# Level products of a chunked recurrence as two 64-row tiles per head pair, pool weights as 64x64 tiles

## The chip, the cores and the metric

One core of one Trainium2 chip. The metric is the time of one execution in microseconds (us) on the device. Engines are named as in the profile: PE (TensorE, with PEld for its weight loads), DVE (VectorE), ACT (ScalarE), POOL (GpSimd), SP (SyncE, which issues the DMAs).

## What is computed

One layer of a hybrid decoder on 2048 tokens of width 1024. The part that the change touches is the gated recurrence (four heads of 64) and the pooling mixer. The recurrence works in chunks of 64 tokens with a decay between each pair of tokens of a chunk:

```python
def step(state, inp):                       # one chunk, all heads
    q_, k_, v_, g_ = inp
    b = jnp.cumsum(g_, axis=2)
    o_inter = jnp.einsum('bhck,bhkv->bhcv', q_ * jnp.exp(b), state)
    diff = b[:, :, :, None, :] - b[:, :, None, :, :]
    decay = jnp.where(causal, jnp.exp(jnp.where(causal, diff, 0.0)), 0.0)
    scores = jnp.einsum('bhik,bhjk,bhijk->bhij', q_, k_, decay)
    o = o_inter + jnp.einsum('bhij,bhjv->bhiv', scores, v_)
    ...
# pooling mixer: y = einsum('bsgc,gcd->bsgd', pooled, w_grp), four groups of 64 channels
```

Around it stand the input projection (16 column tiles of 128), sliding-window attention (8 heads of 64), an output projection, and a gated feed-forward layer of width 2816 with a short convolution.

## The kernel before, in words

Tokens are worked in four blocks of 512. `one_block(0, True)` is written out and also loads and splits the weights; blocks 1 to 3 run as one loop body. Each block goes through input projection with the recurrence's and the attention's small products between its units, output projection, and feed-forward layer. Each engine runs its own program in the order in which the code is written; nothing schedules them, and they meet at semaphores.

Large products are three matmuls of 512 columns (high*high, high*low, low*high) at L606 to L608 (weights stationary) and L631 to L633 (activations stationary). They are of type f32r. The small products are plain float32, and each such matmul stands as two instructions in the trace, with a weight load (LDWEIGHTS) of its own.

**The level products.** The scores inside a chunk come from six levels, of halves of 32, 16, 8, 4, 2 and 1 tokens: within each group of 2w tokens the keys of the first half meet the queries of the second. On DVE `level_sub` (L1491) writes the differences of the cumulative decay to `ZB`, ACT takes exponentials (L1119, L1120), `level_mul` multiplies the second halves by the queries into `ZR` (L1500) and the first halves by the keys into `ZB` (L1503), `level(o)` on PE makes the product (L704), and `level_take` copies it under a mask into `A` (L1520). The 128 partitions hold two heads of 64. To get two heads' products from one matmul over 128 rows, `ZR` is block-diagonal: for each group of 128 tokens it has 128 columns, 64 for each head, and zeros in the other head's half. L1500 thus runs twice a level, on 64 partitions each, and the zeros are written once a block (L1570). A level has 8 matmuls (4 token tiles by 2 head pairs), 16 instructions. `level(0)` (L709, 2 columns) makes the diagonal.

In PE's order the levels stand between the units of the input projection: levels 0 and 1 ahead of unit 7, level 2 ahead of unit 8, level 3 ahead of unit 9, level 4 ahead of unit 10, level 5 behind it and followed by `chunk_states` (L739, 64x64 tiles), level 6 between `scores(0)` and `scores(1)` (L724, whole array, then L728, tiles of 64 rows by 128 columns). `recurrence` follows (L804, whole array; L813, 64x64 tiles). In block 0 `ada_rows` (L548, tiles of 32 columns) runs after units 7, 8, 9 and 10, hence just ahead of levels 2, 3, 4 and 5.

**Pooling.** `pooling` runs two matmuls of 512 columns with a block-diagonal `PW` (L793), into banks 6 and 7 of `ps`, between output units 1 and 2; ACT (L1080) and DVE (L1469, L1470) turn the result into operands of output unit 3.

Of the kernel before, what the change touches and what calls it, by code (L numbers as in the profile page):

```python
# [14 lines left out]
P = 128  # L15
D = 1024
S = 2048
BT = 512
# [53 lines left out]

ACT_STEPS, DVE_STEPS, UP_STEPS = 28, 105, 16

# [23 lines left out]
def hymba_block(nc, x, c, w_ada, b_ada, g_pre_mix, g_post_mix, w_in, hg_norm, pool_w, pool_scale,  # L98
# [19 lines left out]
    with ctx:  # L118
# [83 lines left out]
        ZB = sb("ZB", [P, 2, 2 * BT], fp32, early)  # L202
        ZR = sb("ZR", [P, 2, 2 * TT, P], fp32, early)
        early.close()
# [9 lines left out]
        def fb(name, shape, dt=fp32):  # L214
# [25 lines left out]
              quarter(A[:].rearrange("p t h n -> p (t h n)")), AQ[:], quarter(ZB[:].rearrange("p a n -> p (a n)")),  # L240
              quarter(ZR[:].rearrange("p a b n -> p (a b n)")), AWQK[:], AWT[:], AWG[:])
        DG = AWT[:].rearrange("p k (a n) -> p (k a) n", n=P)
# [285 lines left out]
        def _(pe):  # L528
# [63 lines left out]
            def one_block(b, first):  # L592
# [95 lines left out]
                def level(o, tok):  # L688
# [11 lines left out]
                    for t in range(TT):  # L700
                        for j in range(2):
                            if o:
                                col = (2 * (t % 2) + j) * P
                                ins = mm(ps[:, 4 + 2 * (o % 2) + t // 2, col:col + P],  # L704
                                         ZB[:, (o - 1) % 2, j * BT + t * P:j * BT + t * P + P],
                                         ZR[:, (o - 1) % 2, j * TT + t, :], start=True, stop=True)
                            else:
                                col = 4 * t + 2 * j
                                ins = mm(ps[:, 4, col:col + 2], R[:, j, t * P:t * P + P], hsel[:], start=True, stop=True)  # L709
# [79 lines left out]
                def pooling():  # L789

                    fenced(s["pool_ready"], b + 1)
                    for a in range(2):
                        ins = mm(ps[:, 6 + a, :], PW[:, a, :], R[:, a, :], start=True, stop=True)  # L793
                    ins.then_inc(s["pool_mm"], 1)
# [582 lines left out]
        def _(dve):  # L1377
# [80 lines left out]
            def one_block(b, first):  # L1458
# [35 lines left out]
                def level_mul(l):  # L1494
                    w = LEVELS[l]
                    dve.wait_ge(s["lev_exp"], b * 12 + 2 * l + 2)
                    z, q, k = (y.rearrange("p (n w) -> p n w", w=2 * w) for y in (ZB[:, l % 2, :], flat(Q), flat(K)))
                    for par in range(2):
                        r = slice(64 * par, 64 * par + 64)
                        step(tt(ZR[r, l % 2, :, r].rearrange("p a (n w) -> p a n w", w=w),  # L1500
                                z[r, :, w:2 * w].rearrange("p (a n) w -> p a n w", a=2 * TT),
                                q[r, :, w:2 * w].rearrange("p (a n) w -> p a n w", a=2 * TT), ALU.mult))
                    tt(z[:, :, 0:w], z[:, :, 0:w], k[:, :, 0:w], ALU.mult).then_inc(s["z_ready"], 1)  # L1503

                def level_take(o):
# [9 lines left out]
                    for g in range(2):  # L1515
                        src = ps[:, 4 + 2 * (o % 2) + g, :].rearrange("p (a n w) -> p a n w", a=8, w=w)
                        dst = A[:, 2 * g:2 * g + 2, :, :].rearrange("p t h (n w) -> p (t h) n w", w=2 * w)[:, :, :, w:2 * w]
                        m = hgmask[:, o - 1, :].rearrange("p (n w) -> p n w", w=w)\
# [26 lines left out]
                def window_sums(a):  # L1545
# [21 lines left out]
                    .then_inc(s["kdd"], 1)  # L1567
                for par in range(2):

                    step(ts(ZR[64 * par:64 * par + 64, :, :, 64 * (1 - par):64 * (1 - par) + 64]  # L1570
                            .rearrange("p a b n -> p (a b) n"),
                            ident[64 * par:64 * par + 64, 64 * (1 - par):64 * (1 - par) + 64].unsqueeze(1)
                            .to_broadcast([64, 4 * TT, 64]), 0.0, None, ALU.mult))
                dve.wait_ge(s["q_softplus"], b + 1)
# [206 lines left out]
```

## Time and profile before

| | |
|---|---|
| time of the kernel before | 2347.45 us, median of 3 (2346.28 to 2348.02) |
| the profiled execution | 2343.45 us, its span 2341.7 us |
| PE busy | 2275.6 us (97%), weight loads 1837.2 us |
| DVE busy | 1256.7 us (54%) |
| ACT, POOL busy | 772.3 us (33%), 229.4 us (10%) |
| mean granted TensorE clock | 0.992 |

A row of the chain of work gives start, length and line of each piece of the chain that ended last. For PE a piece runs from the end of the instruction before to its own end, so it is what that instruction added. The single durations of matmuls and weight loads are longer, since they overlap.

### The profile page before, as it was taken

The numbers are of one execution on the slowest core, as the hardware profiler recorded it, in microseconds if no ns is written. First come the engines' busy times: TensorE is split into PE (matmuls) and PEld (weight loads), VectorE is DVE, ScalarE is ACT, GpSimd is POOL, SyncE is SP. The second block draws the span as 40 slices with busy tenths as digits, with TensorE's granted clock in tenths as the row PEclk, the third lists the DMA queues.
The fourth block names the chain that finished last, engine by engine and source line by source line (L and its number), as shares of the span: only waits on it lengthen the run. The fifth ranks groups of instructions, "written<-read, shape, count | busy, mean of one in ns | idle before, by whom it ended". The sixth has DMA issues, their size and how long they took to land.

```text
span 2341.7 us, 33056 instructions
## 1 busy us (share of the span) xinstructions
PE 2275.6 (97%) x11291; PEld 1837.2 (78%) x11307; DVE 1256.7 (54%) x2145; ACT 772.3 (33%) x1500; POOL 229.4 (10%) x151
## 2 busy tenths in 40 slices
PE   6999899999999999999999999999999999999997
PEld 4776688788788778888888778888888877888886
DVE  3648484675766555152556745334355665515345
ACT  3535433343344432121134532113024344212212
POOL 2322244444300000000000000000000000000000
PEclk9999999999999999999999999999999999999999
DMA  9963688878563446555564254655546334655555
GB/s 362 353 223 137 223 293 301 283 272 300 212 256 112 144 145 249 187 191 197 188 221 150 73 198 167 233 194 196 196 163 235 109 144 156 226 193 197 194 187 193
DMA packets 115396, 483.14 MB, mean 206 GB/s; under 512 B 7999, under 2 KB 38985, under 8 KB 69705
## 3 DMA queue, kind: packets, MB, share of 16 engines
q1 hardware_dynamic: 115273, 481.53, 56.8%
q8 instruction: 73, 1.20, 0.2%
q14 instruction: 50, 0.41, 0.1%
HBM read 378.74 MB, written 102.76 MB: 206 GB/s over the span
## 4 chain that ended last, share of the span: by engine, by line
PE 90%; DVE 5%; issue 1%; DMA 1%; SPq 1%; ACT 1%; DVEq 0%; ACTq 0%
PE ps L606 18%; PE ps L608 18%; PE ps L607 18%; PE ps L631 8%; PE ps L633 8%; PE ps L632 8%; PE ps L704 2%; PE ps L728 1%; PE ps L839 1%; PE ps L827 1%; PE ps L670 1%; PE ps L548 1%; PE ps L804 1%; SPq L291 1%; DMA AWT<-in_w_ada_dram 1%
## 5 line engine op out<-in xcount | busy, mean ns | idle before, releaser
L606 PE MATMUL ps<-hTh,wt 128*128 128x512 f32 x1920 | 758.4, 395 | 12.9 <-DVE hTl L1470 8.7
L608 PE MATMUL ps<-hTh,wt 128*128 128x512 f32 x1920 | 748.4, 390 | 0.0
L607 PE MATMUL ps<-hTl,wt 128*128 128x512 f32 x1920 | 748.1, 390 | 0.0
L606 PEld LDWEIGHTS ps<-hTh,wt 128*128 128x128 f32 x1920 | 360.9, 188 | 105.5 <-issue 26.8
L608 PEld LDWEIGHTS ps<-hTh,wt 128*128 128x128 f32 x1920 | 360.7, 188 | 76.3
L607 PEld LDWEIGHTS ps<-hTl,wt 128*128 128x128 f32 x1920 | 361.2, 188 | 71.5
L1704 DVE TENSOR_SCALAR cv<-ub,CW 128x512 f32<-128x512 f32 x176 | 98.2, 558 | 472.5 <-ACT ub L1315 458.0
L1315 ACT ACTIVATE ub<-ps 128x512 f32<-128x512 f32 x176 | 105.3, 598 | 689.7 <-PE ps L608 689.7
L631 PE MATMUL ps<-wt,pTh 128*128 128x512 f32 x704 | 275.1, 391 | 1.9 <-ACT T L1082 1.9
L633 PE MATMUL ps<-wt,pTh 128*128 128x512 f32 x704 | 274.0, 389 | 0.0
L632 PE MATMUL ps<-wt,pTl 128*128 128x512 f32 x704 | 273.9, 389 | 0.0
L511 POOL TENSOR_TENSOR wt<-raw,wt 128x1024 fp32r<-128x1024 f32 x88 | 214.6, 2446 | 402.7 <-ACT wt L989 363.1
L1706 DVE SCALAR_TENSOR_TENSOR cv<-ub,CW,cv 128x512 f32<-128x512 f32 x176 | 162.0, 920 | 26.8 <-DVE halo L1705 26.8
L1707 DVE SCALAR_TENSOR_TENSOR cv<-ub,CW,cv 128x512 f32<-128x512 f32 x176 | 143.1, 813 | 24.8
L631 PEld LDWEIGHTS ps<-wt,pTh 128*128 128x128 f32 x704 | 132.2, 188 | 29.3 <-issue 2.3
L633 PEld LDWEIGHTS ps<-wt,pTh 128*128 128x128 f32 x704 | 132.2, 188 | 27.6
L632 PEld LDWEIGHTS ps<-wt,pTl 128*128 128x128 f32 x704 | 132.2, 188 | 27.0
L1743 DVE TENSOR_TENSOR Y<-Y,ps 128x512 f32<-128x512 f32 x64 | 43.3, 687 | 170.8 <-PE ps L633 170.8
L989 ACT ACTIVATE wt<-raw 128x1024 fp32r<-128x1024 f32 x92 | 95.1, 1036 | 58.7 <-PE ps L633 41.1
L1325 ACT ACTIVATE pTh<-P 128x512 f32 (+1 forms) x88 | 55.3, 628 | 155.7 <-DVE P L1713 155.7
L1500 DVE TENSOR_TENSOR ZR<-ZB,Q 64x512 f32<-64x512 f32 x48 | 35.1, 730 | 73.5 <-ACT ZB L1120 72.3
L1718 DVE TENSOR_TENSOR pTl<-P,pTh 128x512 f32 x88 | 60.6, 688 | 13.6 <-ACT pTh L1325 13.6
(243 smaller groups left out, 2350.3 us busy)
## 6 DMA issues: line engine op xcount, KB each, us to landing
wt<-split_w SPq DMA_DIRECT2D x268, 1024.0 KB, 4.8
split_w<-wt SPq DMA_DIRECT2D x88, 1024.0 KB, 7.0
raw<-in_w_up_dram SPq DMA_DIRECT2D x22, 1024.0 KB, 9.6
XT<-in_w_ada_dram SPq DMA_DIRECT2D x10, 1024.0 KB, 11.5
XN<-in_x_dram SPq DMA_DIRECT2D x5, 2048.0 KB, 9.2
raw<-in_w_in_dram SPq DMA_DIRECT2D x8, 1024.0 KB, 13.7
XR<-in_x_dram SPq DMA_DIRECT2D x4, 2048.0 KB, 10.3
raw<-in_w_down_dram SPq DMA_DIRECT2D x8, 1024.0 KB, 9.2
```

The source lines that it names most:

```text
L511: pool.tensor_tensor(lo, src, hi.bitcast(fp32), ALU.subtract).then_inc(s["w_lo"], 1)
L606: mm(ps[:, bank, :], w, hTh[:, k, :], start=(k == 0), stop=False)
L607: mm(ps[:, bank, :], w, hTl[:, k, :], start=False, stop=False)
L608: ins = mm(ps[:, bank, :], wl[:, slot, k, :], hTh[:, k, :], start=False, stop=(k == KD - 1))
L631: mm(ps[:, 4 * n + t, :], h, flat(wh, j), start=f, stop=False)
L632: mm(ps[:, 4 * n + t, :], l, flat(wh, j), start=False, stop=False)
L633: ins = mm(ps[:, 4 * n + t, :], h, flat(wl, j), start=False, stop=e)
L989: act.activation(hi, src, ACT.Copy).then_inc(s["w_hi"], 1)
L1315: act.activation(ub[:, u, 2:], ps[:, u, :], ACT.Copy).then_inc(s["acc_taken"], 1)
L1704: up(ts(cv[:, u, :], ub[:, u, 2:], tap(2), tap(3), ALU.mult, ALU.add))
L1706: up(stt(cv[:, u, :], ub[:, u, 1:BT + 1], tap(1), cv[:, u, :], ALU.mult, ALU.add))
L1707: stt(cv[:, u, :], ub[:, u, 0:BT], tap(0), cv[:, u, :], ALU.mult, ALU.add)\
```

## The change

`ZR` loses its zero half: it is 64 columns for each token tile and head pair, with head 0 on partitions 0 to 63 and head 1 on 64 to 127. `level_mul` writes it with one instruction on 128 partitions. The L1570 zeroing is gone. On PE each matmul over 128 rows with 128 moving columns becomes two over 64 rows with 64 moving columns, one in each half of the rows, with weights of 64x128; the two heads of a pair write two different banks, where before the banks went by token tiles. `level_take` reads and writes the same number of elements in the new order. `pooling` runs four matmuls on diagonal 64x64 tiles instead of two; both tiles of a pair write the same bank, on different partitions. A buffer of the first block's loads (`AWZ`) takes the place that it had in `ZR`.

```diff
@@ level(), PE
-    col = (2 * (t % 2) + j) * P
-    ins = mm(ps[:, 4 + 2 * (o % 2) + t // 2, col:col + P],
-             ZB[:, (o - 1) % 2, j * BT + t * P:j * BT + t * P + P],
-             ZR[:, (o - 1) % 2, j * TT + t, :], start=True, stop=True)
+    col = (2 * t + j) * 64
+    for par in range(2):
+        r = slice(64 * par, 64 * par + 64)
+        ins = mm(ps[:, 4 + 2 * (o % 2) + par, col:col + 64],
+                 ZB[r, (o - 1) % 2, j * BT + t * P:j * BT + t * P + P],
+                 ZR[r, (o - 1) % 2, j * TT + t, :], start=True, stop=True)
@@ pooling(), PE
-    ins = mm(ps[:, 6 + a, :], PW[:, a, :], R[:, a, :], start=True, stop=True)
+    for q in range(2):
+        r = slice(64 * q, 64 * q + 64)
+        ins = mm(ps[r, 6 + a, :], PW[r, a, r], R[r, a, :], start=True, stop=True)
@@ level_mul(), DVE
-    for par in range(2):
-        r = slice(64 * par, 64 * par + 64)
-        step(tt(ZR[r, l % 2, :, r]..., z[r, :, w:2 * w]..., q[r, :, w:2 * w]..., ALU.mult))
+    step(tt(ZR[:, l % 2, :, :].rearrange("p a (n w) -> p (a n) w", w=w),
+            z[:, :, w:2 * w], q[:, :, w:2 * w], ALU.mult))
@@ level_take(), DVE
-    dst = A[:, 2 * g:2 * g + 2, :, :].rearrange("p t h (n w) -> p (t h) n w", w=2 * w)[:, :, :, w:2 * w]
+    dst = A[:].rearrange("p t h n -> p (t h) n").rearrange("p (a par) (n w) -> p par a n w", par=2, w=2 * w)\
+        [:, g, :, :, w:2 * w]
@@ one_block(), DVE
-    for par in range(2):
-        step(ts(ZR[64 * par:64 * par + 64, :, :, 64 * (1 - par):64 * (1 - par) + 64]..., 0.0, None, ALU.mult))
```

Nothing changes its place in any engine's order. On PE, in the loop body of blocks 1 to 3, before unit 9's first products, level 3 of before (`REGISTER_ALU` rows are waits on a register's value):

```order
1797 L697 REGISTER_ALU
1798 L704 MATMUL ps<-ZR,ZB 128x128 x8
1799 L649 REGISTER_ALU
1800 L606 MATMUL ps<-hTh,wt 128x512
1801 L607 MATMUL ps<-hTl,wt 128x512
```

and of the change:

```order
1797 L700 REGISTER_ALU
1798 L709 MATMUL ps<-ZR,ZB 128x64 x16
1799 L652 REGISTER_ALU
1800 L609 MATMUL ps<-hTh,wt 128x512
1801 L610 MATMUL ps<-hTl,wt 128x512
```

The neighbours stay; eight products of 128 columns are sixteen of 64. On PE at level 6, between the attention's scores (identity and mask L724, keys L728), before:

```order
1870 L724 MATMUL ps<-bmask,identb 128x512 x2
1871 L728 MATMUL ps<-KT,AQ 128x256 x4
1872 L782 ISA
1873 L693 REGISTER_ALU
1874 L704 MATMUL ps<-ZR,ZB 128x128 x8
1875 L724 MATMUL ps<-bmask,identb 128x512 x2
1876 L728 MATMUL ps<-KT,AQ 128x256 x4
```

and with the change:

```order
1870 L729 MATMUL ps<-bmask,identb 128x512 x2
1871 L733 MATMUL ps<-KT,AQ 128x256 x4
1872 L787 ISA
1873 L696 REGISTER_ALU
1874 L709 MATMUL ps<-ZR,ZB 128x64 x16
1875 L729 MATMUL ps<-bmask,identb 128x512 x2
1876 L733 MATMUL ps<-KT,AQ 128x256 x4
```

Here the level stands behind products of 64 rows, whose shape it now shares, and ahead of a product on the whole array. On PE at the pooling, between output units 1 and 2, before and then with the change:

```order
2078 L633 MATMUL ps<-wt,ATT 128x512
2079 L896 REGISTER_ALU
2080 L793 MATMUL ps<-R,PW 128x512 x2
2081 L864 REGISTER_ALU
2082 L631 MATMUL ps<-wt,hTh 128x512
```

```order
2078 L636 MATMUL ps<-wt,ATT 128x512
2079 L903 REGISTER_ALU
2080 L800 MATMUL ps<-R,PW 64x512 x4
2081 L871 REGISTER_ALU
2082 L634 MATMUL ps<-wt,hTh 128x512
```

Two products on the whole array are four on quarters of it, between products on the whole array.

## Rows read from the trace of the kernel before

**Rows 1.** The page: busy times, and the chain's shares by engine.
```profile
PE 2275.6 (97%) x11291; PEld 1837.2 (78%) x11307; DVE 1256.7 (54%) x2145; ACT 772.3 (33%) x1500; POOL 229.4 (10%) x151
...
PE 90%; DVE 5%; issue 1%; DMA 1%; SPq 1%; ACT 1%; DVEq 0%; ACTq 0%
```

**Rows 2.** The chain in block 1, levels 0, 1, 3, 5 (start, us, what).
```profile
690.04 1.68 PE ps L709 x16
691.73 1.89 PE ps L704 x16
693.62 0.23 PE ps L606
...
706.83 1.79 PE ps L704 x16
708.62 0.23 PE ps L606
...
723.16 1.79 PE ps L704 x16
724.95 1.14 PE ps L739 x62
```

**Rows 3.** The chain in block 1 from the chunk states to the recurrence.
```profile
726.08 0.43 PE ps L606
...
733.58 1.06 PE ps L728 x8
734.64 0.03 issue
734.67 2.02 PE ps L704 x16
736.70 0.43 PE ps L724 x2
...
746.04 1.09 PE ps L813 x64
747.14 0.43 PE ps L606
```

**Rows 4.** Groups of PEld by form (rows by columns of the load; busy us, mean ns).
```profile
L704 PEld LDWEIGHTS ps<-ZR,ZB 128*128 128x128 f32 x384 | 47.0, 196 | 6.7 <-issue 5.7
...
L728 PEld LDWEIGHTS ps<-KT,AQ 64*128 64x128 f32 x256 | 22.0, 186 | 15.0 <-issue 13.5
L839 PEld LDWEIGHTS ps<-PT,VA 128*64 128x64 f32 x256 | 15.6, 136 | 10.7 <-issue 5.8 <-DVE ATT L1542 0.4
...
L739 PEld LDWEIGHTS ps<-VH,KDT 64*64 64x64 f32 x256 | 4.3, 134 | 0.5
```

**Rows 5.** Timeline of PEld, 733.505 to 733.6 us.
```profile
733.51 0.19 PEld L728 LDWEIGHTS ps<-KT,AQ 64*128 64x128 f32 x2 [0.42 <-issue]
```

**Rows 6.** Groups of DVE by form (count, busy us, mean ns, idle before).
```profile
L1500 DVE TENSOR_TENSOR ZR<-ZB,Q 64x512 f32<-64x512 f32 x48 | 35.1, 730 | 73.5 <-ACT ZB L1120 72.3
...
L1503 DVE TENSOR_TENSOR ZB<-ZB,K 128x512 f32<-128x512 f32 x24 | 16.6, 693 | 0.8
...
L1570 DVE TENSOR_SCALAR ZR<-ident 64x1024 f32<-64x1024 f32 x8 | 7.7, 961 | 0.1
```

**Rows 7.** Timeline of DVE in block 1: level 3's operands, and the states.
```profile
700.92 1.41 DVE L1500 TENSOR_TENSOR ZR<-ZB,Q 64x512 f32<-64x512 f32 x2 [1.68 <-ACT ZB L1120]
702.36 0.69 DVE L1503 TENSOR_TENSOR ZB<-ZB,K 128x512 f32<-128x512 f32 x1
...
730.99 3.45 DVE L1599 SCALAR_TENSOR_TENSOR SS<-SS,EB,ps 128x64 f32<-128x64 f32 x11 [0.18 <-DVE SS L1599]
```

**Rows 8.** The chain in block 1 at the pooling.
```profile
802.36 1.72 PE ps L793 x4
804.08 0.23 PE ps L631
```

**Rows 9.** Timeline of DVE behind the pooling in block 1.
```profile
806.44 0.69 DVE L1470 TENSOR_TENSOR hTl<-T,hTh 128x512 fp32r<-128x512 f32 x1
```

**Rows 10.** The chain in block 0, levels 2 to 5.
```profile
106.92 1.98 PE ps L704 x16
110.28 0.79 PE ps L557 x8
...
117.66 0.60 SPq L291
...
118.30 12.66 DMA AWG<-in_w_ada_dram
...
132.94 3.30 PE ps L704 x16
...
146.30 1.98 PE ps L704 x16
```

**Rows 11.** Timeline in block 0, from level 2 to that load: ACT, POOL, SP.
```profile
111.10 0.17 ACT L1058 ACTIVATE MOD<-ps 128x4 f32<-128x4 f32 x1 [3.52 <-PE ps L557]
...
112.39 2.39 POOL L511 TENSOR_TENSOR wt<-raw,wt 128x1024 fp32r<-128x1024 f32 x1 [8.42 <-ACT wt L989]
...
114.81 0.83 SPq L325 DMA_DIRECT2D split_w<-wt  x2
```

**Rows 12.** Stretches: busy of PE, PEld, DVE, ACT, POOL, then PEclk, the granted clock.
```profile
265.00:271.30 6.30, 3.56 (x19) 2.61 (x19) 6.03 (x7) 6.04 (x17) 0.00 (x0) 1.00 0.78 257
834.20:840.50 6.30, 3.63 (x20) 2.67 (x18) 5.85 (x8) 5.85 (x17) 0.00 (x0) 1.00 0.57 199
...
272.20:275.60 3.40, 3.40 (x18) 3.26 (x16) 1.13 (x2) 1.19 (x2) 0.00 (x0) 0.50 0.00 0
840.00:843.40 3.40, 2.87 (x24) 2.59 (x24) 1.23 (x2) 2.05 (x5) 0.00 (x0) 1.00 0.74 287
1398.60:1402.00 3.40, 3.03 (x14) 3.03 (x15) 1.07 (x2) 1.33 (x4) 0.00 (x0) 0.50 0.65 270
1958.40:1961.80 3.40, 3.15 (x15) 3.15 (x16) 0.95 (x2) 1.21 (x4) 0.00 (x0) 0.50 0.62 236
```

More of the change, by code:

```diff
@@ L71, in ada_use @@
     return slot, sum(s == slot for p in ADA_SLOT[:e] for s in p) + 1
-ACT_STEPS, DVE_STEPS, UP_STEPS = 28, 105, 16
+ACT_STEPS, DVE_STEPS, UP_STEPS = 28, 97, 16
 def place(u):
@@ L202, in hymba_block @@
         ZB = sb("ZB", [P, 2, 2 * BT], fp32, early)
-        ZR = sb("ZR", [P, 2, 2 * TT, P], fp32, early)
+        wide = ExitStack()
+        AWZ = sb("AWZ", [P, 4, 512], fp32, wide)
+        wide.close()
+        ZR = sb("ZR", [P, 2, 2 * TT, P // 2], fp32, early)
         early.close()
@@ L240, in hymba_block @@
               quarter(A[:].rearrange("p t h n -> p (t h n)")), AQ[:], quarter(ZB[:].rearrange("p a n -> p (a n)")),
-              quarter(ZR[:].rearrange("p a b n -> p (a b n)")), AWQK[:], AWT[:], AWG[:])
+              AWZ[:], AWQK[:], AWT[:], AWG[:])
         DG = AWT[:].rearrange("p k (a n) -> p (k a) n", n=P)
@@ L1497, in level_mul @@
                     z, q, k = (y.rearrange("p (n w) -> p n w", w=2 * w) for y in (ZB[:, l % 2, :], flat(Q), flat(K)))
-                    for par in range(2):
-                        r = slice(64 * par, 64 * par + 64)
-                        step(tt(ZR[r, l % 2, :, r].rearrange("p a (n w) -> p a n w", w=w),
-                                z[r, :, w:2 * w].rearrange("p (a n) w -> p a n w", a=2 * TT),
-                                q[r, :, w:2 * w].rearrange("p (a n) w -> p a n w", a=2 * TT), ALU.mult))
+                    step(tt(ZR[:, l % 2, :, :].rearrange("p a (n w) -> p (a n) w", w=w),
+                            z[:, :, w:2 * w], q[:, :, w:2 * w], ALU.mult))
                     tt(z[:, :, 0:w], z[:, :, 0:w], k[:, :, 0:w], ALU.mult).then_inc(s["z_ready"], 1)
@@ L1567, in one_block @@
                     .then_inc(s["kdd"], 1)
-                for par in range(2):
[L1570 to L1573, printed above, removed]
                 dve.wait_ge(s["q_softplus"], b + 1)
```

## The prediction, made before the change was run

> **What bounds the kernel now.** I read the page first. PE is busy 97% of the span, and 90% of the chain of work that ended last is PE [rows 1]. So PE's own order is the path, and the question is what each product adds to it. I then read the chain in block 1, where nothing but PE stands in it from the levels to the recurrence. There a level adds 1.79 us for 16 instructions, 0.112 us each, and the projection's next product, L606, adds its ordinary 0.23 us [rows 2]. Level 0 adds 1.68 us for 16, or 0.105 us each, although only 2 columns move through the array where the other levels move 128 [rows 2]. So the moving columns do not set the pace of a small product: what both have in common is a weight load of 128 columns. The loads' durations say by what they go: 186 ns for 64 rows by 128 columns and 196 for 128 by 128, but 136 for 128 by 64 and 134 for 64 by 64 [rows 4]. Columns count, rows do not.
>
> DVE is busy 54% [rows 1]. In the levels it stands idle ahead of L1500, 72.3 us in all, until ACT's exponentials come [rows 6], and none of it is in the chain there. Its result is early: level 3's operands are done at 703.05 (702.36 + 0.69) [rows 7], and PE comes to that level at 706.83 [rows 2].
>
> **Part 1, DVE.** 48 instructions of 730 ns (35.1 us) become 24 on 128 partitions. The same form exists in L1503, 693 ns [rows 6]: 16.6 us. The zeroing, 7.7 us, goes. DVE loses 26.2 us of 1256.7, some 6.5 a block. Worth on the path: nothing at levels 2 to 5, where the operands are already 3.8 us early in the example above. The one place where DVE comes close is the chunk states, which end at 734.44 (730.99 + 3.45) [rows 7], when PE waits for them ahead of level 6 at 734.67 [rows 3]. The last L1500 stands ahead of them on DVE, so they come 0.7 us earlier. I count that under level 6. `level_take` moves as many elements as before: nothing.
>
> **Part 2, the steady rate of a level.** A level becomes 32 instructions, 16 pairs. The two of a pair use different rows. Do they overlap? L728 is the nearest row: 64 rows by 128 columns of weights, two row halves, 256 columns moving. Two such loads stand within 0.19 us, the length of one [rows 5], and eight products take 1.06 us, 0.13 each [rows 3]. At twice L704's columns they could not take less than 0.22 each if they ran one behind another. So pairs overlap. Each pair still needs a load of 128 columns, the same as one instruction of before. I take 0.112 us a pair, hence 1.79 us a level: **no gain and no loss** at the steady rate. The ends: half of it (0.9 us) if rows counted in a load, twice (3.58 us) if the two ran in turn; both are rivals below.
>
> **Part 3, changing the shape of the tiles.** Here the change costs. Wherever PE goes from tiles to the whole array, the next product adds 0.43 us, not 0.23: behind L739 and behind L813 [rows 3]. Behind an untiled level it adds 0.23 [rows 2]. Leaving tiles costs **0.20 us**. Entering a new shape: a level behind L728 takes 2.02 us [rows 3] where one behind L608 takes 1.79 [rows 2], so 0.23 us, in which the first load and the first moving columns are laid bare. With 64 columns moving for 128 about 0.05 of it goes, and 0.03 may be waiting (the issue row ahead of it [rows 3]). I take **0.14 us** for entering tiles of 64 rows, with 0 and 0.23 as ends. The Trainium skill has this as a rule, in "TensorEngine Tiling (Array Packing)", section Key Properties: changing the tiling mode drains the engine, while going from tile to tile does not. The trace agrees, with the 0.20 and 0.23 us just read. By the same rule level 6 saves its entry behind L728, as the next list has it from the rows; were tiles of any shape free to change, level 5 and L739 would share one drain and the sum would be 0.6 us less.
>
> In blocks 1 to 3:
> - Level 1 stands behind level 0, and its 1.89 us already show 0.10 us of a bare load [rows 2]. Entering adds 0.04, leaving 0.20: 0.24.
> - Levels 2, 3 and 4 stand between products on the whole array: 3 x 0.34 = 1.02.
> - Level 5 enters (0.14); it was followed by a change of shape before (L739) and still is: 0.14.
> - Level 6 follows L728, whose shape it now has: its 2.02 us fall to 1.79, -0.23, and the states that PE waited for are earlier. But L724 on the whole array follows; leaving costs 0.17 there, a little under 0.20 since its own load is of bf16 (a guess between 0.14 and 0.20). Together -0.06.
> - Pooling: four instructions of 512 columns take 1.72 us, 0.43 each [rows 8]. Eight on diagonal quarters, in pairs that overlap, take the same; entering and leaving add 0.34. The split of its result ends at 807.13 (806.44 + 0.69) [rows 9]; output unit 3 begins 24 products of 0.227 us behind 804.08 [rows 8], at 809.5. 2.4 us of cover hold the added time, the more so as both shift together.
>
> That is 1.68 us a block, 5.04 for three.
>
> Block 0 differs, as L548's tiles of 32 columns stand ahead of levels 2 to 5: those levels pay for a change of shape already (1.98 us at 106.92 and 146.30 [rows 10], 0.19 over 1.79) and save the 0.05 of the shorter columns. Level 1: 0.24. Level 2: -0.05 + 0.20 = 0.15; it is not hidden, since L557 behind it, at 110.28, leads through ACT, POOL and SP [rows 11] to the load at 118.30. Level 3 lies under that load of 12.66 us [rows 10]: 0. Level 4 runs at half clock, 3.30 us [rows 10]: 0.2, within 0.15 and 0.3. Level 5: -0.05. Level 6: -0.06. Pooling 0.34. Together 0.82.
>
> **The sum:** 5.04 + 0.82 = 5.9 us. Against the profiled execution's 2343.45 us that is 2349.3. The median of the runs is 4.0 us above that execution, a difference that the change leaves alone: 2347.45 + 5.9 = **2353.3 us**, 0.25% slower. Bounds: with every entry at nothing (16 places at 0.14 and four at 0.04 less) the sum is 3.5 us; with 0.23 at the 16 places it is 7.3.
>
> **Rivals.**
>
> *The pool's pairs run in turn* (slower still). The two quarters of a pair write one bank. No row shows that: L728, L739 and L813 send different row halves to different banks. If they must take turns, 8 x 0.43 = 3.44 us for 1.72, so 1.72 x 4 = 6.9 us more: 2360.2. For it: nothing in the trace, either way. Against: the two write different partitions, and L739 with two column halves in one bank overlaps (62 in 1.14 us [rows 2]). The Trainium skill, in "TensorEngine Tiling (Array Packing)", section Gotcha 1: PSUM Pressure, says that different row tiles cannot use one PSUM bank at the same time. No run here shows whether the hardware then waits.
>
> *Rows count in a load* (the other side: faster). Then a pair takes 0.056 us, a level 0.9, and 23 levels on the path save 0.89 each, 20.5 us: 2347.45 + 5.9 - 20.5 = 2332.9. It decides from the point where a pair takes less than 0.10 us. Against it stands 186 ns for a load of 64 rows beside 134 with half the columns [rows 4], and level 0's 0.105 us at 2 columns. The Trainium skill, in "TensorEngine Tiling (Array Packing)", section Theoretical Speedup, gives up to 2x for a small dimension of 64 or less, which is this case; by the same rows the trace speaks against it here.
>
> *The pairs of a level run in turn.* 23 levels x 1.79 = 41 us: 2394. Against: the overlap of L728 [rows 3, 5].
>
> *The clock hides it* (no measurable change). Ahead of the feed-forward layer PE is busy only 3.56 of 6.3 us in block 0, and 3.63 of 6.3 in block 1 [rows 12]. In block 0 the granted clock is then 0.50 (1.2 GHz) for a stretch of 3.4 us, and so in blocks 2 and 3; in block 1 it stays 1.00 (2.4 GHz) [rows 12]. Whether it falls after much the same idle is thus a matter of when that comes, and the change moves when. A stretch at half clock costs up to 1.7 us of PE. Two or three of them gone give back 3 to 5 us: 2349 or so. One more gives 2355.
>
> **How the numbers follow.** My forecast has 0.69, with a range of its own of 2350.5 to 2356.5. The pool in turn has 0.13, the clock 0.11, rows in a load 0.04, level pairs in turn 0.03. The range of 8 in 10 reaches from 2349.5, the clock's case, to 2360.5, the pool's. A measurement of this kernel tells 0.2% (4.7 us) from no change, so the border to slower is 2352.1, only 1.2 us under my forecast. Of the forecast's 0.69 I put 0.48 above it and 0.20 below, of the clock's case all between, with 0.01 of luck left to faster. Slower 0.48 + 0.13 + 0.03 = 0.64, faster 0.04 + 0.01 = 0.05, within 0.2% 0.31.
>
> **What would show it.** In the chain of the profile after: levels 2 to 4 at 1.93 us each with the next L606 line at 0.43; level 6 near 1.79 and the L724 behind it about 0.6 for the two; pooling near 1.86 us and the next product 0.43; DVE some 26 us less busy, with more idle ahead of `ZR`. Pooling at 3.5 us shows the bank. A level under 1.5 or over 2.3 us shows my steady rate wrong. If the rows are as I say and the time is still 2349 or less, I look for the stretches at half clock, and then for a wait that DVE's relief took away which I read as covered.

## The result, and the profile after

| | before | after |
|---|---|---|
| median of five executions | 2347.45 us (2345.70 to 2348.02) | 2357.54 us (2355.51 to 2362.76) |
| ratio, interval of 95% | | 1.0049 [1.0036, 1.0062] |
| the profiled execution, its span | 2343.45, 2341.7 us | 2355.51, 2353.8 us |
| its granted clock, mean | 0.992 | 0.989 |
| granted clock, mean of the five executions | | 0.988 |

The change makes the kernel 0.49% slower: 10.1 us between the medians, 12.1 between the profiled executions. It lies in the predicted range (2349.5 to 2360.5), but above the predicted time of 2353.3 and outside the forecast's own range (2350.5 to 2356.5): 5.9 us were forecast and some 10 came.

The page after, beside [rows 1] and [rows 6] (a group's row: engine, operation, tiles and count | busy us, mean ns | idle time ahead of it and what ended it):

```profile
PE 2288.7 (97%) x11691; PEld 1843.3 (78%) x11707; DVE 1231.8 (52%) x2113; ACT 771.9 (33%) x1500; POOL 228.9 (10%) x151
...
L1505 DVE TENSOR_TENSOR ZR<-ZB,Q 128x512 f32<-128x512 f32 x24 | 16.6, 692 | 98.1 <-ACT ZB L1127 97.7
```

DVE is 24.9 us less busy, and its idle time ahead of this line, now L1505, has grown from 72.3 to 97.7 us: what DVE saves it waits for ACT, one for one. The prediction had 26.2 us less; `level_mul`'s multiplication into `ZB`, an instruction whose form did not change, takes 18.7 us in all where it took 16.6.

The level products are now L709, level 0 is L714, the projection's products L609 to L611, the masks L729, the pooling L800. The chain of work in block 1 (start, length, line), beside [rows 2, 3, 8]:

```profile
693.51 1.68 PE ps L714 x16
695.19 1.93 PE ps L709 x32
697.12 0.43 PE ps L609
...
702.79 1.93 PE ps L709 x32
704.72 0.43 PE ps L609
...
727.87 1.93 PE ps L709 x32
729.81 1.14 PE ps L744 x62
...
738.42 1.06 PE ps L733 x8
739.49 1.73 PE ps L709 x32
741.22 0.54 PE ps L729 x2
...
806.95 1.86 PE ps L800 x8
808.82 0.43 PE ps L634
```

Level by level this is close to what was forecast. The difference of these rows against those of before is 0.24 for level 1, 3 x 0.34 for levels 2 to 4, 0.14 for level 5, 1.73 - 2.02 + 0.54 - 0.43 = -0.18 for level 6 and 0.34 for the pooling: 1.56 us a block, where the prediction had 1.68. And the weight loads show why a level became no faster: 64 rows of 128 columns take 197 ns, where 128 rows of 128 took 196 [rows 4].

```profile
L709 PEld LDWEIGHTS ps<-ZR,ZB 64*128 64x128 f32 x768 | 47.7, 197 | 8.6 <-issue 8.4
```

Three blocks at 1.56 us and block 0 at some 0.8 make 5.5 us of shape changes. More than half of the 12.1 us between the profiled executions is still to be found. Most of it is in the same lines, at other places. Block 3 and block 0 after (the same view):

```profile
1815.92 1.68 PE ps L714 x16
1817.60 2.99 PE ps L709 x32
1820.59 0.72 PE ps L609
1821.31 0.43 PE ps L610
```

```profile
117.93 1.41 SPq L294
...
119.39 12.73 DMA AWG<-in_w_ada_dram
...
132.16 1.93 PE ps L551 x8
134.10 3.61 PE ps L709 x32
137.71 0.72 PE ps L609
...
139.28 1.71 PE ps L684 x8
...
142.27 0.86 PE ps L560 x8
```

The same place of before, behind [rows 10]:

```profile
138.52 0.78 PE ps L557 x8
```

Stretches of both kernels (busy of PE, PEld, DVE, ACT, POOL, then the granted clock). After, levels 0 and 1 of block 3, which begin at 1815.9:

```profile
1814.00:1818.20 4.20, 4.20 (x37) 3.87 (x37) 0.35 (x1) 2.13 (x4) 0.00 (x0) 1.00 0.28 62
1818.20:1825.00 6.80, 6.80 (x35) 5.72 (x34) 5.78 (x6) 2.02 (x4) 0.00 (x0) 0.50 0.27 116
```

Block 0 behind the wait for `AWG`, first after, then before:

```profile
128.70:135.50 6.80, 5.27 (x30) 1.90 (x32) 0.81 (x2) 0.60 (x1) 0.00 (x0) 0.50 1.05 392
135.50:142.40 6.90, 6.90 (x39) 6.10 (x37) 2.56 (x3) 0.00 (x0) 0.00 (x0) 0.51 0.04 17
```

```profile
128.80:135.60 6.80, 5.73 (x29) 2.93 (x22) 1.05 (x2) 0.60 (x1) 0.00 (x0) 0.50 1.03 384
135.60:142.50 6.90, 6.90 (x46) 6.11 (x46) 2.54 (x3) 2.66 (x6) 1.87 (x1) 1.00 0.01 5
```

The granted clock falls to 0.50 (1.2 GHz) in the midst of busy PE work in block 3, 0.6 us into level 1, and in block 2 too (3.4 us from 1258.5, 0.5 us behind the end of level 1). In block 0 both kernels fall to 0.50 while PE waits for `AWG` and runs `ada_rows`; before comes back to 1.00 behind level 4, and after stays at 0.50 for twice as long. Outside the last 13 us of the span, before has 23.9 us at 1.2 GHz and after 41.0.

I priced each such stretch by its own rows: every PE product in it against its length at 2.4 GHz. That makes 8.5 us before and 14.2 after, 5.7 more. This is an estimate; in experiments with more such stretches the terms come to 0.5 to 2 us more than the span.

The rows put the 5.7 us at places. Behind the landing of `AWG` it is 2.7 us, of which about 0.3 is the change of shape. At levels 0 and 1 it is about 1.6 us in block 2 and 3.0 in block 3. The other stretches, which lie partly elsewhere than before, give back some 1.3.

With the shapes' 5.5 that makes 11.2. The remaining 0.9 us is the wait for `AWG`: from the end of `ada_rows` to the landing it is 13.30 us before (130.96 - 117.66) and 14.19 after (132.12 - 117.93). In the ten experiments it is 14.2 to 14.8 us, also where nothing in block 0's levels 2 to 5 is tiled (14.77 in `e_level0_twice`). So the tiles are not needed for it, and the profiled execution of before was quick there.

**A price for the mean clock.** The mean clock of an execution is recorded with its time. I took the 93 of the experiments' kernels and of the runs of before beside them. One line through all, with an offset for each kernel and, for before, for each of its three sets, has a slope of 1.34 us for 0.001 of the mean clock and leaves 1.3 us. With it the kernels can be put at one clock, 0.992. This is an estimate, and good to about 1 us. Before stands at 2345.1, 2345.2 and 2344.2 then, and after, by its five times, at 2352.3: some 7.1 us. The rest, some 3 to 4 us, is clock.

### The profile page after: what moved, and what is told of

It reads as the page before. It is cut to its first block, busy times and chain, and to the rows that moved or that the text cites. A ratio compares the mean times of both kernels' runs of the same rounds, so it can differ in the third digit from the quotient of the medians.

```text
span 2353.8 us, 33796 instructions
## 1 busy us (share of the span) xinstructions
PE 2288.7 (97%) x11691; PEld 1843.3 (78%) x11707; DVE 1231.8 (52%) x2113; ACT 771.9 (33%) x1500; POOL 228.9 (10%) x151
## 4 chain that ended last, share of the span: by engine, by line
PE 90%; DVE 5%; issue 1%; DMA 1%; SPq 1%; ACT 1%; DVEq 0%; ACTq 0%
PE ps L609 18%; PE ps L611 18%; PE ps L610 18%; PE ps L634 8%; PE ps L635 8%; PE ps L636 8%; PE ps L709 2%; PE ps L733 1%; PE ps L846 1%; PE ps L834 1%; PE ps L673 1%; PE ps L551 1%; PE ps L811 1%; SPq L294 1%; PE ps L684 1%
## 5 line engine op out<-in xcount | busy, mean ns | idle before, releaser
L609 PE MATMUL ps<-hTh,wt 128*128 128x512 f32 x1920 | 760.2, 396 | 11.5 <-DVE hTl L1477 8.3
L611 PE MATMUL ps<-hTh,wt 128*128 128x512 f32 x1920 | 749.7, 390 | 0.0
L609 PEld LDWEIGHTS ps<-hTh,wt 128*128 128x128 f32 x1920 | 361.5, 188 | 104.8 <-issue 24.7
L611 PEld LDWEIGHTS ps<-hTh,wt 128*128 128x128 f32 x1920 | 361.5, 188 | 76.7
L1505 DVE TENSOR_TENSOR ZR<-ZB,Q 128x512 f32<-128x512 f32 x24 | 16.6, 692 | 98.1 <-ACT ZB L1127 97.7
```

The costliest lines, as they stand in the source:

```text
L609: mm(ps[:, bank, :], w, hTh[:, k, :], start=(k == 0), stop=False)
L611: ins = mm(ps[:, bank, :], wl[:, slot, k, :], hTh[:, k, :], start=False, stop=(k == KD - 1))
```

## The experiments

Each kernel ran four to ten times beside the kernel before, in three groups, each on a chip of its own. The text quoted under a heading is what was expected before that run. The column "1.2 GHz" is the sum of the stretches at 0.50 in the profiled execution, without the end of the span; "cost" what they took from PE, priced as above. The first group is the four rows from `e_split01` to `e_levels_only`, the second `e_after_again` and the three from `e_pe_only` to `e_quarters`, the third the last two rows. The figures of before stand in the order of the groups.

| kernel | median (range), us | ratio to before | at clock 0.992 | 1.2 GHz, cost |
|---|---|---|---|---|
| before, beside the three groups | 2345.55, 2347.04, 2345.70 | | 2345.1, 2345.2, 2344.2 | 23.9, 8.5 |
| after | 2357.54 | 1.0049 [1.0036, 1.0062] | 2352.3 | 41.0, 14.2 |
| e_after_again | 2355.70 (2355.11 to 2356.73) | 1.0038 [1.0024, 1.0051] | 2351.5 | 44.4, 14.4 |
| e_split01 | 2352.78 (2350.4 to 2355.9) | 1.0034 [1.0021, 1.0047] | 2350.6 | 27.3, 8.5 |
| e_level1_only | 2359.02 (2358.59 to 2364.73) | 1.0061 [1.0048, 1.0074] | 2354.0 | 47.8, 16.6 |
| e_not_level1 | 2353.52 (2349.68 to 2357.2) | 1.0033 [1.0023, 1.0042] | 2348.9 | 41.0, 11.2 |
| e_levels_only | 2354.01 (2349.54 to 2357.86) | 1.0032 [1.0019, 1.0045] | 2349.2 | 47.8, 15.6 |
| e_pe_only | 2357.53 (2351.03 to 2362.1) | 1.0048 [1.0034, 1.0062] | 2350.7 | 34.1, 11.5 |
| e_block0_level4 | 2353.24 (2349.41 to 2358.22) | 1.0024 [1.0013, 1.0036] | 2349.4 | 51.2, 16.6 |
| e_quarters | 2330.87 (2328.51 to 2335.32) | 0.9933 [0.992, 0.9947] | 2329.2 | 30.7, 9.4 |
| e_quarters_split | 2330.17 (2327.81 to 2330.98) | 0.9929 [0.9915, 0.9942] | 2329.2 | 34.1, 9.7 |
| e_level0_twice | 2373.00 (2366.63 to 2375.0) | 1.0117 [1.0101, 1.0132] | 2362.9 | 44.4, 17.5 |

The theory: PE pays for each change of the tiles' shape, and the rest of the loss is the clock, which falls or stays down where tiled level products run. Its rivals: the fallen stretches are chance, DVE's or the pooling's part of the change is behind the rest, or a term of the shapes is larger than its row.

### Level 1 away from level 0

On the kernel after:

```diff
     level(0, 2)
-    level(1, 2)
-    unit(7)
+    unit(7, {4: lambda: level(1, 2)})
```

> The changed kernel with one edit: level 1's products leave their place right behind level 0 and stand in the middle of projection unit 7 (behind 4 of its 8 k-tiles). Theory 1 (the quiet stretch): half of the loss of 10 us comes from the granted clock, which falls to 1.2 GHz because level 0 (1.68 us with 2 columns moving) and the tiled level 1 (1.93 us) stand in a row. Then no stretch at half clock is left at level 0 or 1 in blocks 1 to 3, and the time is 2353 to 2355 us. Theory 2 (phase): stretches at half clock fall where they do by the time at which idle comes, not by this pair; then this edit changes nothing systematic and the time stays 2356 to 2359 us with stretches at half clock at either level in some blocks. Both expect the level's own products to take 1.93 us plus 0.20 us for leaving the tiles.

The chain in block 1:

```profile
693.97 1.34 PE ps L714 x12
695.31 0.35 PE ps L609
...
698.20 1.93 PE ps L709 x32
700.13 0.43 PE ps L609
```

Level 1 costs the same wherever it stands (1.93 and 0.43), and leaving level 0's two columns for the large product adds 0.12. No stretch at 0.50 lies in or behind levels 0 and 1 in any block, and the cost of the clock is that of before, 8.5 us. The profiled execution is 5.1 us shorter than that of after. The medians say less: 2352.78, just under the first theory's 2353 to 2355, against 2357.54 and 2355.70, with intervals of the ratio that overlap.

### One level alone, and all but that one

Both start from the kernel before; the levels named read 64-row halves of its block-diagonal operand, the others are whole. DVE's multiplication and the pooling stay as before.

```diff
@@ level()
-    if o:
+    if o in (1,):            # e_not_level1: (2, 3, 4, 5, 6)
+        col = (2 * t + j) * 64
+        for par in range(2):
+            r = slice(64 * par, 64 * par + 64)
+            ins = mm(ps[:, 4 + 2 * (o % 2) + par, col:col + 64],
+                     ZB[r, (o - 1) % 2, j * BT + t * P:j * BT + t * P + P],
+                     ZR[r, (o - 1) % 2, j * TT + t, r], start=True, stop=True)
+    elif o:
```

> The kernel before with one part of the change: level 1 alone runs as two products of 64 rows per head pair, read out of the block-diagonal operand, which stays with all its work on DVE; its result is copied in the new bank order. The chain of the change prices this at 0.04 + 0.20 us a block, 1.0 us in all. Theory 1 (quiet stretch of level 0 and tiled level 1): in some of blocks 1 to 3 the clock falls to 1.2 GHz there, and the time is 2351 to 2353.5 us. Theory 2 (phase, or any tiled product alike): 2348 to 2349.5 us.

> The counterpart: the kernel before with levels 2 to 6 tiled and level 1 and the pooling as they were, the block-diagonal operand and its DVE work kept. By the price of changing shape: 5.9 - 1.0 (level 1) - 1.4 (pooling) = 3.5 us over before, 2351. Theory 1: that is all, since level 1 is whole behind level 0: 2350.5 to 2352, no stretch at half clock at level 0 and 1 in blocks 1 to 3. Theory 2 (any tiled level adds its share of the clock's loss, 4 us over 6 levels): 2353.5 to 2355.

By the sum's terms, level 1 alone should cost 1.0 us and the others 3.5. At equal clock the others do: 2348.9 against 2345.1, 3.8. Their profiled execution has no fall at levels 0 and 1 either. But the median, 2353.52, is 8.0 us over before, above the first theory's range and at the edge of the second's, and equal clock takes out just what the two differ in. Of the ten executions five took 2349.7 to 2351.8 us at a clock of 0.989 to 0.991 and five 2355.2 to 2357.2 at 0.987; the profiled one is of the first five. The mean clock, 0.9887, is as low as that of the whole change (0.9878 and 0.9888). So a clock loss of some 3.7 us is there with level 1 whole, and more of it than block 0's stretch. Where it lies in the longer executions no profile shows.

Level 1 alone missed both ranges. It costs 8.9 us at equal clock and 13.5 in the medians, more than the whole change. Its rows say where. The first 60 us have a stretch of 17.1 us at 1.2 GHz (from 34.4), and PE has fallen 4.4 us behind before at 51 us, ahead of any level. One fall (3.4 us from 1826.4) begins as level 1 of block 3 ends. The largest part is a wait that no theory had: 3.6 us of "issue" or more at each of the two jumps back to the head of the loop (up to 1217.7 and 1782.1), where before has 0.5 at most. Each has a stretch at 1.2 GHz beside it, of which this is the first:

```profile
1218.80:1222.20 3.40, 3.40 (x10) 2.62 (x9) 3.37 (x4) 0.50 (x3) 0.00 (x0) 0.51 0.64 251
```

The kernel can't be read as the price of level 1.

### Levels without the pooling

The kernel after, with the pool's products of before:

```diff
-    for q in range(2):
-        r = slice(64 * q, 64 * q + 64)
-        ins = mm(ps[r, 6 + a, :], PW[r, a, r], R[r, a, :], start=True, stop=True)
+    ins = mm(ps[:, 6 + a, :], PW[:, a, :], R[:, a, :], start=True, stop=True)
```

> The changed kernel with the pooling back as two products on the whole array. Both theories: 4 x 0.34 us less than the change, 2355.5 to 2357, and the pooling's four instructions at 1.72 us again with 0.23 us for the next product.

2354.01 us, under the 2355.5 to 2357 that was expected. At equal clock it stands 4.1 us over before, where the terms without the pooling's 1.4 give 4.5. The pooling in block 0 (now L798) is back at its old rows:

```profile
236.05 1.72 PE ps L798 x4
237.77 0.23 PE ps L634
```

Its profiled execution is as long as that of after (spans of 2353.7 and 2353.8 us), with 15.6 us of clock for 14.2. The pooling itself is settled by the rows, 1.86 and 0.43 us with the change. Its pairs, on one bank, overlap.

### The change again

> The changed kernel unchanged, once more, beside the next ones on one chip. Shapes cost 5.9 us, which a run pays at any clock; the rest is clock. 2354 to 2359 us, median 2356. Theory 1a: the tiled level 4 in block 0 again leaves the clock at 1.2 GHz for about 13.7 us from 129 us on, where before it was 6.8. Theory 1b: in some of blocks 1 to 3 the clock falls at level 0 and 1.

2355.70 us, 1.8 under the first set. The stretches at 1.2 GHz are nearly the same in sum (44.4 and 41.0 us), but not in place. Block 2's levels stay at 1.00 this time, and in block 3 the fall (3.4 us from 1820.3) begins as level 1 ends. The stretch from 38.5 us, in the loads at the start, is 10.2 us for 3.4 the first time, with the same program. In block 0 the long stretch is there again, 13.7 us. So that one belongs to the program; those at levels 0 and 1, and the length of the one at the start, change from execution to execution.

### PE's part without DVE's

All six levels as in the diff of `e_level1_only`, `if o in (1, 2, 3, 4, 5, 6)`; `level_mul` and the zeroing stay as before, and so does the pooling.

> The PE part of the change without the DVE part: levels 1 to 6 as tiles of 64 rows, read out of the block-diagonal operand, which keeps its two multiplications per level and its zeroing; pooling as before. If DVE's 26 us of relief are worth nothing, as predicted, this equals the change less the pooling's 1.4 us: 2353 to 2356. If the relief was worth something, this is slower than the changed kernel.

2357.53 us, 1.5 above the range that was expected, with executions from 2351.0 to 2362.1. DVE is busy 1255.1 us, as before. Against `e_levels_only`, which differs in DVE's work alone, it stands at 2350.7 to 2349.2 at equal clock; the medians, of two groups, are 3.5 us apart, at a mean clock of 0.9874 and 0.9885. The profiled executions, with their clock's cost taken off, are 2349.3 - 11.5 = 2337.8 and 2353.7 - 15.6 = 2338.1 us. 23 us of DVE work are worth nothing that these runs can show, at most about 1.5 us at equal clock.

### Block 0's level 4 left whole

`e_pe_only` with one exception:

```diff
-    if o in (1, 2, 3, 4, 5, 6):
+    if o in (1, 2, 3, 4, 5, 6) and not (first and o == 4):
```

> As the run with the PE part alone, but in block 0 level 4 stays one product on the whole array. Theory 1a (while the clock is at 1.2 GHz, a tiled level does not count as enough activity to bring it back, a whole one does): the stretch at half clock around 129 us is 6.8 us again, and the time is 2.5 to 3.5 us under that of the PE part alone: 2350.5 to 2352.5. Theory 2 (the length of that stretch has nothing to do with the tiles): no difference beyond 0.3 us from one shape less, and a stretch of 13.7 us.

The stretch at 1.2 GHz behind the wait for `AWG` is 6.8 us again:

```profile
133.30:140.10 6.80, 5.61 (x24) 2.25 (x25) 1.06 (x2) 0.60 (x1) 0.00 (x0) 0.50 1.01 380
140.10:147.00 6.90, 6.90 (x48) 6.15 (x47) 2.53 (x3) 2.21 (x5) 1.42 (x1) 1.00 0.01 4
```

The chain there (the landing of `AWG` is the end of the first row, at 136.38):

```profile
123.56 12.82 DMA AWG<-in_w_ada_dram
...
143.47 0.78 PE ps L557 x8
```

From the landing to L557 it is 7.09 us, where `e_pe_only` has 10.00. That is 2.9 us back on the path, of which about 0.3 is the change of shape. Over all kernels this splits cleanly. With level 4 whole in block 0 (before, `e_level1_only`, `e_level0_twice`, this one) the stretch is 6.8 us, four of four. With it in pairs of 64-row tiles (after, again, `e_split01`, `e_not_level1`, `e_levels_only`, `e_pe_only`) it is 13.7, six of six; with quarter tiles 10.2 and 13.7. The time from the landing to L557 (L560) is 6.8 to 7.6 us in the four and 10.0 to 10.2 in the six. The median is 4.3 us under that of `e_pe_only`, at equal clock 1.3. At 2353.24 it is above the range of the first theory, 2350.5 to 2352.5, and the intervals of the two ratios overlap; the stretch and the rows decide, not the median. The same profile has a fall at levels 0 and 1 of block 0, where level 1 took 3.03 us, so that its clock cost is no less in sum.

### Quarters instead of halves

A product of 64 rows still loads 128 columns: the keys of two chunks. Keys of one chunk meet only queries of the same chunk, and the copy's mask drops the rest. On `e_levels_only`, four tiles of 64 by 64 with 32 moving columns take the place of two; the products between the two chunks of a group of 128 tokens are left out, and no result uses them.

```diff
+    pe.sem_inc(s["pe_fence"], 1)
     for par in range(2):
         r = slice(64 * par, 64 * par + 64)
-        ins = mm(ps[:, 4 + 2 * (o % 2) + par, col:col + 64],
-                 ZB[r, (o - 1) % 2, j * BT + t * P:j * BT + t * P + P],
-                 ZR[r, (o - 1) % 2, j * TT + t, :], start=True, stop=True)
+        for c_ in range(2):
+            k0, q0 = j * BT + t * P + 64 * c_, 32 * c_
+            ins = mm(ps[64 * c_:64 * c_ + 64, 4 + 2 * (o % 2) + par, col + q0:col + q0 + 32],
+                     ZB[r, (o - 1) % 2, k0:k0 + 64],
+                     ZR[r, (o - 1) % 2, j * TT + t, q0:q0 + 32], start=True, stop=True)
```

(The first line, a step of a semaphore, stands ahead of the loops, once a level.)

> The changed kernel (pooling as before), but each level product is cut further into 64x64 tiles: a head's 64 rows by one chunk of 64 tokens, with the 32 query columns of that chunk moving. The products between different chunks, which the mask discards, are left out. If the pace of a level is its weight load by columns, four tiles share one load of 64 columns and a level takes 16 rounds of 0.058 us, 0.93, plus 0.14 for entering: 1.05 instead of 1.93. Leaving costs 0.20, and level 5 has no change of shape behind it. Sum against before per later block: levels 1 to 4 at 1.05 + 0.20 against 1.79 to 1.89, -0.6 each; level 5 1.05 - 1.79 - 0.10; level 6 1.05 + 0.2 + 0.2 against 2.02. That is about -3.8 us a block: 2331 to 2335 us, before a loss at the clock of 0 to 5 us. If rows counted in a load or four tiles did not overlap, a level would stay at 1.8 us or more and the time at 2350 or above.

The chain in block 1, and the group of its loads:

```profile
698.14 1.06 PE ps L712 x64
699.21 0.43 PE ps L609
...
720.63 1.07 PE ps L712 x64
721.70 1.01 PE ps L747 x62
```

```profile
L712 PEld LDWEIGHTS ps<-ZR,ZB 64*64 64x64 f32 x1536 | 25.4, 138 | 10.1 <-issue 10.0
```

A level with twice the instructions takes 1.06 us for 1.93 (1.79 before), since a load of 64 columns is 138 ns where one of 128 is 197, and four of them share the array: 1.065 / 16 is 0.067 us for a round of four. The moving columns were halved too, but they do not set this pace: `chunk_states`, with 64 moving columns on the same tiles, took 1.14 us for 64 instructions before, and level 0, with 2 moving columns and 128 loaded, 1.68 for 16. The way out is the same 0.20, and `chunk_states` (now L747, the same 64x64 tiles) behind level 5 falls from 1.14 to 1.01. The median is 2330.87 us, 16.2 under its runs of before: this version beats both kernels. And its mean clock, 0.9906 (0.9916 in the next experiment), is that of before (0.9910 and 0.9907 beside them), though all six levels are tiled and have the most instructions of all.

### Quarters, with level 1 away from level 0

> The quarters kernel (level products as 64x64 tiles, 32 query columns moving, the products between the two chunks of a group of 128 tokens left out), with level 1 moved from behind level 0 into the middle of unit 7. It adds an entry and a way out that level 0 shared in part: by the sum's terms at most 0.1 to 0.3 us a block, 0.4 to 1.2 in all. Theory 'the row of small products of levels 0 and 1 costs clock': the quarters kernel showed one stretch at 1.2 GHz just behind level 1 of block 2, which goes; 1.7 us back in that execution, and a mean of several executions 1 to 2 us under 2330.9, at 2329 to 2330. Theory 'these falls are luck that the order of the products does not set': no gain, 2331 to 2332 us.

2330.17 us, between the two theories' ranges, and 2329.2 at equal clock like the other. The mean is 2329.8 for the other's 2331.1, one of whose five executions took 2335.3. No stretch at 1.2 GHz lies at levels 0 and 1; the other had one just behind them, and the clock's cost is the same in sum (9.7 and 9.4). The gain asked for, 1 to 2 us, can't be told from nothing.

### Level 0 twice, on the kernel before

```diff
+    pe.wait_ge(s["qk_ready"], b + 1)
+    for t in range(TT):
+        for j in range(2):
+            mm(ps[:, 5, 4 * t + 2 * j:4 * t + 2 * j + 2], R[:, j, t * P:t * P + P], hsel[:], start=True, stop=True)
     level(0, 2)
     level(1, 2)
```

> The kernel before, with the eight two-column products of level 0 issued twice in a row (16 more instructions a block); the levels stay whole, on the block-diagonal operand. By their row, 0.105 us each, the second set adds 1.68 us a block, 6.7 in all: 2347 + 6.7 = 2353.7 us. Theory 'small products in a row let the granted clock fall': in the kernels with a tiled level 1 behind level 0 the clock fell to 1.2 GHz there in some of the blocks; if few moving columns over a few us do that whatever the shape of the tiles, then level 0 twice and level 1 (5.3 us in a row) make it fall in at least one or two of the blocks 1 to 3, level 1 then takes 3 us or more there, and the time is 1.7 to 6 us above 2353.7. Theory 'it is the tiled shape': the clock stays at 1.00 through levels 0 and 1 in every block, level 1 takes 1.89 us, and the time is 2352 to 2355 us.

The chain in block 3 (L769 and L709 are level 0, L704 level 1), and its stretch:

```profile
1827.76 1.68 PE ps L769 x16
1829.44 1.79 PE ps L709 x16
1831.22 3.13 PE ps L704 x16
1834.36 0.43 PE ps L606
```

```profile
1831.60:1835.00 3.40, 3.40 (x16) 3.22 (x15) 2.91 (x3) 0.53 (x1) 0.00 (x0) 0.50 0.10 34
```

A whole level, no tiles of 64 rows, and the clock falls in it all the same, in blocks 2 and 3 (2.55 and 3.13 us for level 1); in blocks 0 and 1 it stays (1.89). So the fall needs no tiled shape: it came in two of four rows of small products that take 5.4 us at full clock. The time, 2373.00 us, is far above both theories' ranges, the higher of which ends at 2359.7. The wait at the jump back is here too, twice, the first time so (with 6.8 us at 1.2 GHz from 1217.2):

```profile
1214.83 4.11 issue
1218.94 0.58 PE ps L606
1219.53 0.43 PE ps L607
```

The profiled execution is 23.2 us longer than that of before. Of it 7.2 are the added products (1.68 + 1.79 - 1.68, four times), some 7 the two waits, and 9.0 the clock (17.5 less 8.5). With the 1.5 us longer wait for `AWG` the terms come to 25, so they are 1 to 2 us too high. The other executions are longer still, at a mean clock of 0.984 or 0.985 for the 0.988 of this one.

## Why the prediction was right, and what it mis-sized

- **The bound, PE's own order:** right. 90% of the chain is PE before and after.
- **The steady rate:** right. A pair of 64-row tiles goes in the time of one whole product, and the load of 64 by 128 takes 197 ns for 196. Both rivals of this step fall: rows don't count in a load (a level would be 0.9 us), and the pairs of a level don't take turns (3.58). One link was unsound though it held: that L728 could not go one behind another in less than 0.22 us was taken from "twice L704's columns", while the same text finds that columns don't set L704's pace. The row that bears it out is the pool's 0.43 us for 512 columns, 0.21 for 256.
- **Changing shape:** right in size. 0.14 for entering and 0.20 for leaving are each in the rows, at levels 2 to 4 and at the pooling; level 5 shows the 0.14. With them the Trainium skill's rule in "TensorEngine Tiling (Array Packing)", section Key Properties, that a change of tiling mode drains the engine, agrees with the rows at 0.34 us for both ways; the rows show the price and not its cause. Level 6 was taken as -0.06 and is -0.18. Its level, which has no way in, takes 1.73 us and not 1.79, so up to 0.06 of what is called entering may be the steady rate.
- **The pool's pairs in turn** (0.13): fell. 1.86 us for eight instructions, and not 3.44. The two tiles of a pair write one bank on different partitions and overlap, where the Trainium skill, in the same page's Gotcha 1: PSUM Pressure, forbids it; measured, it costs nothing here.
- **Rows in a load, so faster** (0.04): fell for 64 by 128. The same page's Theoretical Speedup of up to 2x for a small dimension of 64 or less doesn't come from the rows: two 64-row tiles gained nothing. It comes when the loaded columns are halved as well: 1.79 to 1.06.
- **DVE, worth nothing:** right, by the idle row and by `e_pe_only`.
- **Block 0's level 4 at 0.2 us, within 0.15 and 0.3:** the step that failed. The level itself is +0.31 (3.61 for 3.30), just over the 0.3 that was its upper end. But the products behind it are at 1.2 GHz too now: from the landing of `AWG` to L560 (L557) it is 142.27 - 132.12 = 10.15 us, where before it was 138.52 - 130.96 = 7.56. With L560 a bit longer, that is 2.7 us for the 0.2. With it in the sum the forecast would have been 2355.8. The prediction read the stretch as given and priced the level inside it. It did not ask whether what follows the idle time also decides when the clock comes back. `e_block0_level4` shows that it does: 7.09 us for 10.00.
- **The clock as a rival:** mis-sized, and turned the wrong way. It was put down as luck that could give back 3 to 5 us or take 2. Over the runs it went one way: the mean clock is 0.9878 and 0.9888 in the two sets of after, 0.991 in those of before, and the slope makes that 3 to 4 us. Part of it is block 0's, 2.4 us in a profiled execution. Falls in or just behind levels 0 and 1 are another part: five in 24 blocks where a level 1 in pairs stands right behind level 0 (two inside level 1, three as it ends or up to 0.5 us behind), none in 8 where level 1 is whole and level 0 stands once, none in 4 where it is moved away. The kernels in quarters have one in 4 with level 1 behind level 0, and none in 4 with it moved. Those counts don't prove it, and `e_not_level1` speaks against its being the whole: its mean clock is as low, 0.9887, with level 1 whole. That a row of small products can do it is shown by `e_level0_twice`, two blocks of four.

The sum of shapes, 5.9, compares with 5.5 from the rows and 7.1 or 6.3 at equal clock, which is good to about 1 us. The other 3 to 4 us of the 10 in the medians are the clock, by the estimate.

**What stays open.** Whether pairs of 64-row tiles in level 1 make a fall likelier than the whole level, which lasts nearly as long, isn't shown; the counts are small. Nor is it shown where the clock is lost in the longer executions, since each kernel has one profile, and in five of the eleven it is that of the shortest execution. And why pairs in block 0's level 4 keep the clock down, while the kernels in quarters lose none of their mean clock, I can't say. The wait at the loop's jump is not explained. It appears in `e_level1_only` and `e_level0_twice` (3.6 to 4.1 us), and not in the kernels with more levels tiled, though these have more instructions.

## What to carry to other kernels

Halving the rows of small products buys nothing while each still loads 128 columns; look for a cut of the loaded columns first, as with the two chunks here, and only then pay the 0.34 us for going into tiles and out. Where PE is the bound, read the granted clock around every row of small products and behind every wait, and count as a price of the change what keeps it down. When kernels are put at one clock, what the change did to the clock is taken out with the chance, so read both figures. A difference of a few us in the median is settled only when the stretches at 1.2 GHz of both profiles have been laid side by side.

## What the runs showed of the hardware that I had not expected

- The granted clock falls to 0.50 with PE busy all the time, inside a row of small products. After, PE is busy 4.20 of 4.20 us ahead of the fall at 1818.2 and 6.80 of 6.80 behind it; in `e_level0_twice` it is busy 3.40 of 3.40 from 1831.6. In [rows 12] the falls came behind idle time.
- Once at 0.50 it comes back or not by what PE runs: behind the same wait 6.8 us with level 4 whole and 13.7 in halves, in ten profiles of ten. With quarters it is 10.2 and 13.7. PE is busy 6.90 of 6.90 us in the second half of the long stretch.
- Tiles of different rows that write one bank of `ps` on different partitions run at the same time: eight pooling instructions in 1.86 us, the four whole ones in 1.72.
- Four fp32 instructions on 64 by 64 tiles with 32 moving columns go in 0.067 us (1.065 / 16) and two on 64 by 128 in 0.121 (1.93 / 16), each with the way in; one on the whole array goes in 0.112.
- The head of a loop body cost PE some 4 us (4.11 and 3.75 in `e_level0_twice`, 3.62 and 4.06 in `e_level1_only`) in two kernels that differ from before by a few instructions; before has 0.54 at most.
